# Gated squares added on VectorE, the first two gate tiles in halves, and the value mix begun a step earlier in a two-layer hybrid kernel

## The reference

```python
v = v + (v_first - v) * jax.nn.sigmoid(v0 + (h @ v1) @ v2)     # second layer only
...
y = y.reshape(bsz, s, D_S5) + d_skip.astype(f32) * uf.reshape(bsz, s, D_S5)
y = jax.nn.gelu(y)
y = y * jax.nn.sigmoid(y @ glu_w.astype(f32) + glu_b.astype(f32))
return rmsnorm(y, out_g).astype(u.dtype)
...
x = x + jnp.concatenate([y_rw, y_s5], axis=-1) @ w_out[l]
```

## Time and profile before

| | us |
|---|---|
| median of 3 runs (range) | 3774.73 (3774.5 to 3781.53) |
| profiled execution, its own time | 3779.59 |
| its span, first to last instruction | 3777.9 |
| TensorE busy | 3612.9 (96%) |
| VectorE busy | 2973.0 (79%) |
| ScalarE busy | 1368.3 (36%) |
| GpSimd busy | 711.3 (19%) |

### The profile page before, as it was taken

One profiled execution on the slowest core, in us unless ns is written; L12 is line 12 of the kernel. 1 busy time (PEld: TensorE's weight loads), 2 busy tenths in 40 slices (PEclk: granted clock), 3 DMA queues, 4 the chain that ended last, 5 costly groups with the idle time before them and its releaser, 6 DMA issues. The chain is left out here.

```text
span 3777.9 us, 69540 instructions
## 1 busy us (share of the span) xinstructions
PE 3612.9 (96%) x28530; PEld 3331.1 (88%) x28530; DVE 2973.0 (79%) x5456; ACT 1368.3 (36%) x2066; POOL 711.3 (19%) x592
## 2 busy tenths in 40 slices
PE   8799889999999999999999888999999999999998
PEld 5578767899999999999987776789999999999998
DVE  8577474799998978788876747569999897778887
ACT  3441243433334443333333124343333444333333
POOL 2000000022222124343310000002222212345321
PEclk9899999999999999999999999999999999999999
DMA  6820312388787889999951031238878789899995
GB/s 219 295 73 16 117 51 95 122 273 262 259 265 245 307 326 340 354 373 368 356 190 60 21 120 51 95 107 263 265 253 275 248 293 351 320 355 359 376 353 205
DMA packets 323805, 876.27 MB, mean 232 GB/s; under 512 B 29696, under 2 KB 158848, under 8 KB 315680
## 3 DMA queue, kind: packets, MB, share of 16 engines
q1 hardware_dynamic: 249760, 603.36, 45.8%
q0 software_dynamic: 73728, 268.47, 19.3%
HBM read 746.93 MB, written 124.78 MB: 231 GB/s over the span
## 5 line engine op out<-in xcount | busy, mean ns | idle before, releaser
L2338 POOL DMA_INDIRECT row<-in_peer_u_rows,row_at x256 | 324.4, 1267 | 1695.7 <-DVE row L2595 1012.8
L222 PE MATMUL peer_ps<-peer_h_high,tile_high 128*128 128x384 f32 (+1 forms) x1504 | 510.9, 340 | 0.0
L224 PE MATMUL peer_ps<-peer_h_high,tile_low 128*128 128x384 f32 (+1 forms) x1504 | 508.4, 338 | 0.0
L223 PE MATMUL peer_ps<-peer_h_low,tile_high 128*128 128x384 f32 (+1 forms) x1504 | 508.1, 338 | 0.0
L215 DVE TENSOR_TENSOR tile_low<-peer_tile,tile_high 128x1024 fp32r<-128x1024 f32 x362 | 441.3, 1220 | 62.7 <-ACT tile_high L210 59.7
L2338 POOL DMA_INDIRECT row<-in_peer_v,row_at x256 | 360.5, 1408 | 605.1 <-DVE own_sum L2601 558.3
L222 PE MATMUL peer_ps<-gate_high,tile_high 128*128 128x384 f32 x1360 | 458.6, 337 | 4.9 <-DVE tile_low L215 4.9
L223 PE MATMUL peer_ps<-gate_low,tile_high 128*128 128x384 f32 x1360 | 457.0, 336 | 0.0
L224 PE MATMUL peer_ps<-gate_high,tile_low 128*128 128x384 f32 x1360 | 456.9, 336 | 0.0
L210 ACT ACTIVATE tile_high<-peer_tile 128x1024 fp32r<-128x1024 f32 x362 | 379.8, 1050 | 15.7 <-DMA peer_tile<-in_peer_u 15.7
L210 ACT ACTIVATE gate_high<-weighed 128x384 fp32r<-128x384 f32 x256 | 134.8, 527 | 683.2 <-PE peer_ps L224 392.8
(11 more groups left out here) (528 smaller groups left out, 7919.3 us busy)
## 6 DMA issues: line engine op xcount, KB each, us to landing
peer_tile<-in_peer_u SPq DMA_DIRECT2D x256, 512.0 KB, 4.7
peer_tile<-in_peer_v SPq DMA_DIRECT2D x256, 512.0 KB, 6.6
gates<-gates_out SPq DMA_DIRECT2D x24, 2048.0 KB, 11.6
gates_in<-gates SPq DMA_DIRECT2D x32, 1536.0 KB, 10.9
acts<-up_act SPq DMA_DIRECT2D x240, 192.0 KB, 5.0
act_in<-acts SPq DMA_DIRECT2D x240, 192.0 KB, 6.7
in_w<-in_w_in SPq DMA_DIRECT2D x36, 512.0 KB, 3.2
peer_tile<-in_peer_wq SPq DMA_DIRECT2D x32, 512.0 KB, 4.2
```

Of the source, the lines that this page charges most:

```text
L222: pe.matmul(out, wh, mh, start=first, stop=False)
L223: pe.matmul(out, wh, ml, start=False, stop=False)
L224: return pe.matmul(out, wl, mh, start=False, stop=last)
L2338: pool.indirect_dma_start(row[n % NROW][:, :], None, table, bass.IndirectOffsetOnAxis(ap=row_at[:, n % ROWS:n % ROWS + 1], axis=0)) \
```

## The change

Front, layer 2: the first two of the three steps of the value mix move from step 15 to step 14, that is ahead of the take of tile 15.

Tail, both layers: on TensorE tiles 0 and 1 are each cut in two halves of two planes and interleaved (0 first half, 1 first half, 0 second half, 1 second half). VectorE adds the four squares into plane 0 by three additions, each waiting for the one before (`gated_added`), and one product with ones behind tile 5 takes the place of four behind tile 7. ScalarE rounds the mixed planes after all four gate planes, and VectorE takes their low parts after all four low parts of the gate.

```diff
@@ front, VectorE @@
-                if j == 15:
-                    if layer:
-                        dve.wait_ge(first_loaded.sem, first_loaded.at(16))
-                        link(dve.tensor_tensor(lw[:, :, :], lw[:, :, :], v[:, :, :], ALU.subtract))
-                        dve.wait_ge(v2_taken.sem, v2_taken.at(KH))
-                        link(dve.tensor_tensor(lw[:, :, :], lw[:, :, :], av[:, :, :], ALU.mult))
-                        link(dve.tensor_tensor(v[:, :, :], v[:, :, :], lw[:, :, :], ALU.add))
+                if j == 14 and layer:
+                    dve.wait_ge(first_loaded.sem, first_loaded.at(16))
+                    link(dve.tensor_tensor(lw[:, :, :], lw[:, :, :], v[:, :, :], ALU.subtract))
+                    dve.wait_ge(v2_taken.sem, v2_taken.at(KH))
+                    link(dve.tensor_tensor(lw[:, :, :], lw[:, :, :], av[:, :, :], ALU.mult))
+                if j == 15 and layer:
+                    link(dve.tensor_tensor(v[:, :, :], v[:, :, :], lw[:, :, :], ALU.add))
@@ mixer_tail, TensorE @@
-            def half_tile(j):
+            def half_tile(j, k0=0, k1=KH):
...
-                for k in range(KH):
+                for k in range(k0, k1):
...
-                last.then_inc(summed.sem, 1)
+                if k1 == KH:
+                    last.then_inc(summed.sem, 1)
...
-            for j in range(4):
+            for k0, k1 in ((0, 2), (2, KH)):
+                for j in range(2):
+                    pe.wait_ge(spread_taken.sem, spread_taken.at(j + 1))
+                    half_tile(j, k0, k1)
+            for j in range(2, 4):
                 pe.wait_ge(spread_taken.sem, spread_taken.at(j + 1))
                 half_tile(j)
             for j in range(4, 8):
                 pe.wait_ge(skipped.sem, skipped.at(j - 3))
                 half_tile(j)
-            pe.wait_ge(gated.sem, gated.at(KH))
-            for t in range(KH):
-                pe.wait_ge(out_squared.sem, out_squared.at(t + 1))
-                last = pe.matmul(ps[0][:, :], pg.c["ones"][:, :], glu[:, t, :], start=(t == 0), stop=(t == KH - 1))
-            last.then_inc(out_summed.sem, 1)
+                if j == 5:
+                    pe.wait_ge(gated.sem, gated.at(KH))
+                    pe.wait_ge(gated_added.sem, gated_added.at(KH - 1))
+                    pe.matmul(ps[0][:, :], pg.c["ones"][:, :], glu[:, 0, :], start=True, stop=True).then_inc(out_summed.sem, 1)
@@ mixer_tail, ScalarE @@
-                if t == 0:
-                    for k in range(KH):
-                        mixed_high(k)
+            for k in range(KH):
+                mixed_high(k)
@@ mixer_tail, VectorE @@
-                for k in ((), (0, 1), (2, 3), ())[t]:
-                    mixed_low(k)
...
+            for k in range(KH):
+                mixed_low(k)
...
+            for t in range(1, KH):
+                dve.wait_ge(out_squared.sem, out_squared.at(t + 1))
+                if t >= 2:
+                    dve.wait_ge(gated_added.sem, gated_added.at(t - 1))
+                dve.tensor_tensor(glu[:, 0, :], glu[:, 0, :], glu[:, t, :], ALU.add).then_inc(gated_added.sem, 1)
             low(8)
```

More of the change, by code:

```diff
@@ L960, in mixer_tail @@
     mix_made, mix_high, mix_low = pg.counts("mix_made"), pg.counts("rhs_high_made"), pg.counts("rhs_low_made")
-    gated, multiplied = pg.counts("glu_gated"), pg.counts("glu_multiplied")
+    gated, multiplied, gated_added = pg.counts("glu_gated"), pg.counts("glu_multiplied"), pg.counts("glu_squares_added")
     out_squared, out_summed, out_meaned, out_rooted = (pg.counts(f"norm_{n}") for n in ("squared", "summed", "meaned", "rooted"))
@@ L1337, in mixer_tail @@
                  (high_made, len(HALF_TILES)), (low_made, len(HALF_TILES)), (summed, len(HALF_TILES)), (taken, KD),
-                 (glu_high, 2 * KH), (glu_low, KH), (mix_made, KD), (mix_high, KD), (mix_low, KD), (gated, KH), (multiplied, KH),
+                 (glu_high, 2 * KH), (glu_low, KH), (mix_made, KD), (mix_high, KD), (mix_low, KD), (gated, KH), (multiplied, KH), (gated_added, KH - 1),
                  (s_in, 1), (s_taken, 4), *((in_loaded[t], 16) for t in range(4)), (out_squared, KH), (out_summed, 1), (out_meaned, 1), (out_rooted, 1)):
```

## The result

| | before | changed |
|---|---|---|
| median (range), 6 runs each | 3779.85 (3774.5 to 3793.91) | 3751.71 (3744.7 to 3756.41) |
| profiled execution, its own time | 3779.59 | 3745.04 |
| its span | 3777.9 | 3743.3 |
| mean granted clock of TensorE | 0.983 | 0.985 |

The ratio is 0.9923 with a 95% interval of 0.9905 to 0.9941: the changed kernel is faster, by 28 us between the medians. The forecast was 3752.4. It met the time, but not quite the gain: it took 22.3 us off a median of 3774.73, and over six runs that median came out 5 us higher.

A forecast was written before the change was run, and what follows sets the result against it. TensorE was taken to stand waiting for late gate low halves, the mean of squares and layer 2's value mix. 4.2 + 5.8 + 2.0 + 5.8 + 4.5 = 22.3 us off 3774.73 gives 3752.4; range 3746 to 3763.

The forecast's parts named there:

- B: Mean of the gated squares, both tails: one early product for four, tile 4 to tile 11 in 20.1, 5.8 us per layer.
- The 0.1 for the restart behind the old wait: Tail, after TensorE's idle 2.72 ahead of tile 10: a restart loss of 0.1 us that goes with the wait.
- Rival 2: Mean in the tail: additions slip past their 0.7 spare, TensorE waits, 2 us per layer, 3756.4; chance 7%.
- C: End of layer 2's front: two value-mix steps go into VectorE's idle 4.41, gaining 4.5 us.
- A, layer 1: Gated part of layer 1's tail: plane order and halves start the output tiles 4.2 us earlier, given full clock.
- A, layer 2: Gated part of layer 2's tail: plane order and halves start the output tiles 2.0 us earlier.
- the fourth skip sum has to wait for that end: Layer 2's gate: the sum waits for products running until 2303.48, so the gain there is only 2.0 us.
- Rival 1: Gate tiles 0 and 1: alternating accumulators drop TensorE to 1.2 GHz, 4.8 us per layer, 3762; chance 6%.
- Rival 5: Tiles 4 to 19, each layer: the clock falls to 1.2 GHz and stays, 77 us for 32 tiles, slower; chance 4%.
- Rival 4: Whole kernel: half-rate stretches fall elsewhere or a consumer takes the gain back, no visible change, 3768 to 3774; chance 6%.
- The additions: VectorE's three chained sums of gated squares: about 0.72 us each, done before tile 5 ends, no wait.

The follow-up runs named there:

- one late: Kernel before, with VectorE adding the gated squares and one product of ones at the old place behind tile 7: 3775.69 us, ratio 0.999.
- four early: Kernel before, with only the four products of ones moved behind tile 5: 3771.41 us, ratio 0.9973.
- the one where the pause is 1.5 us: Changed kernel with ScalarE's end-of-tail squares for the next norm moved behind the next half-tile split: 3743.66 us, ratio 0.9897 to the kernel before.

## Why the prediction was right, and where it was not

**B, right in its mechanism.** Forecast: additions done 4.8 after tile 4 starts (514.9 less 510.1), no wait, 0.7 to spare, 20.1 for the distance. Measured: 4.83 (511.06 less 506.23), none, 0.7, 20.12. The 0.1 for the restart behind the old wait came too: from tile 11's first product to the end of the last it is 25.14 us in the first profile of the changed kernel for 25.25 in that of before, so 5.8 in all. The two terms behind it hold apart as well: three products by 2.6 (one late against four, and four early against the changed kernel), the wait by 3.1. Rival 2 does not occur; moving the product one tile earlier makes a wait of that kind, 2.0 us.

**C, right.** Forecast 4.5 and an idle time of 2.2; measured 4.4 of idle time gone, 2.28 left, with the front alone and with everything.

**A, layer 1: right in size.** Forecast 4.2 with the assumption that the clock would not fall, since the gaps ahead of it went. Measured 4.4 in the first pair of profiles, no idle time, clock 1.00; on the means of both kernels' profiles (19.2 and 14.8) it is 4.4. Three more kernels have the old gate part, and their layer 1 takes 20.2 to 20.4, with 6.8 us at half the clock that reach over products behind the last low half. Over all six profiles with the old part (19.8) and all four with the new one (14.7) the term is 5.1. So the forecast priced the gate beside a short stretch at half the clock; the longer ones, gone as well, are worth more, and that it stayed as close as this is partly luck of the profile.

**A, layer 2: the mis-sized term.** The step that failed reads "the fourth skip sum has to wait for that end": I took the end of the S5 products from the earlier trace rows as fixed, 5.4 us behind the first skip sum. Two things set that distance: the products themselves and a stretch at half the clock that lay on them in that profile. In the kernel before this did not matter. Its gate takes 18.9 to 19.0 in layer 2 in all three profiles and 18.9 in three more kernels, with 3 to 6.3 us at half the clock inside, because VectorE's chain ended last and the slower products lay beside it. In the changed kernel the chain is short and the products end last: the gate is 14.65 where they run at full clock and 17.0 where they do not. The one gives 4.2 for the term, the other 1.9. My 2.0 was the price of one of the two cases, taken as the only one. On the means (18.9 and 15.8) the term was 3.1 (3.4 over the same six and four profiles as for layer 1: 18.9 and 15.5). Layer 1 is bound the same way: the 498.8 taken for its first product is 3.6 us behind the first skip sum, measured were 3.1 and 3.8, hence 14.6 and 15.0 for a forecast of 14.9.

**The clock.** Rival 1 (alternating accumulators) is out, also with four of them: 0.23 a product at full clock. The Trainium skill, TensorE: Matmul & The Clock Gate, section on psum-queue depth-cycling, ties such oscillation to short idle times between groups of products; the groups here leave none, so no run here contradicts it, and none shows it. Rival 5 is out: tiles 4 to 10 run at 2.75 us each, tiles 11 to 19 at 2.77. Rival 4 in its first form did not come about either; the stretches at half the clock sum to 128.9 us in the first profile of before and 109.1 in that of the changed kernel.

**The additions.** They end 4.83 us after tile 4 starts, where 4.8 was forecast, but the step was priced a little low. The second and the third addition of layer 1 in the changed kernel, behind the first at 508.79:

```profile
509.56 0.69 DVE L1299 TENSOR_TENSOR s_turns<-s_turns 128x512 f32<-128x512 f32 x1
510.36 0.69 DVE L1299 TENSOR_TENSOR s_turns<-s_turns 128x512 f32<-128x512 f32 x1
```

An addition that waits for the one before starts 0.78 and 0.80 after it, not 0.72, about 0.1 behind its end. Four low parts that wait for nothing new (2.49 for x4, each 0.69 long) start 0.60 apart, and so does the low part behind the last addition (510.97). So the three take 2.27 us for the 2.16 of the forecast. The Trainium skill, VectorE: DVE Perf Modes, section "The DRAIN you can't avoid", says that a semaphore between chained steps costs nothing; here a waiting step starts 0.18 to 0.20 later than one that doesn't wait. No run separates the wait itself from the need for the result.

**The total.** The three changed stages gave 23.7 for 22.3. The measured medians differ by 28.1, the profiles' means by 30.8. What lies over the 23.7 is spread over stages whose code is the same. It goes with less time at half the clock and a little less idle time there, but whether that belongs to the change stays open: scatter of single profiles would be enough for part of it, yet the means of seven and seven profiles lean one way. The forecast time was met so closely partly because its base, the median of three runs, lay 5 us under that of six.

## What to carry to other kernels

Before you price an edit from a row, ask whether that stretch could have run at the other clock level, and whether the engine's slowness was hidden there: once the chain beside it is shortened, the same stretch is on the path. Split a late reduction's cost into place and number, since each can be had alone, and push it forward until the wait for its input appears; here one tile decided. A wait ahead of dense matmuls costs more than its length when half the clock follows it.

## What the runs showed of the hardware that I had not expected

- An idle time of TensorE was followed by a stretch at half the clock in some executions and not in others: 4 of 12 behind the 2.7 us ahead of tile 10, 1 of 2 behind the 2.0 us of the product behind tile 4. Behind the 4.34 us between tail and cross attention it seems the rule: in the 13 profiles with that pause each cross attention has 2.9 us or more at half the clock, and in the one where the pause is 1.5 us neither has any. In the tails it costs 1.3 to 1.6 us each time.
- Distances that only the order of the instructions sets, with no stretch at half the clock in them, repeat to 0.02 us (20.12 in ten layers of five profiles), while the same program's time moves by 10 us and more from run to run. Local distances decide between theories where totals do not: the ratios of the parts alone, from ten runs each, have intervals 0.0024 to 0.003 wide, more than the gains themselves.
- In the S5 products, small matmuls of 64 columns in long rows, TensorE stops for 1 to 3 us several times with nothing that it waits for (13.5 us in 8 gaps in the changed kernel). Where the gaps fall moves from profile to profile; their cause was not tried.
